# Token Fourier transform on folded halves, with v rows and gate loads placed differently, in a two-sequence encoder kernel

## The reference

```python
def fourier_mix(f):                      # f: tokens x 512 channels, 8 groups of 64
    fg = f.reshape(B, S, 8, 64)
    return jnp.fft.fftn(fg, axes=(1, 3), norm='ortho').real   # over tokens and over a group's channels

h = x @ w_in                             # f_in, q, k, v, gates
f_branch = fourier_mix(f_in) @ w_fo
a_branch = window_attention(q, k, v, sink) @ w_ao     # 8 heads, 2 kv heads, blocks of 128 tokens
merged = gates[..., :1024] * f_branch + gates[..., 1024:] * a_branch
x = layer_norm(ALPHA * x + merged @ w_out)
# peer: 128*128 = 16384 experts; 8 heads choose 16 each per token
s1, i1 = top_k(...); s2, i2 = top_k(...)              # chosen experts and softmax gates
act = gelu(x . u[eidx]); out = sum(gate * act * v[eidx])
x = layer_norm(ALPHA * x + out + ple)
```

## Time and profile before

| what | us |
|---|---|
| three runs | 3372.45, 3372.86, 3387.92 |
| median | 3372.86 |
| the profiled execution's own time | 3368.09 |
| its span, first to last instruction | 3366.2 |
| PE busy | 3206.8 (95%) |
| DVE busy | 1968.2 (58%) |
| POOL busy | 1866.5 (55%) |
| ACT busy | 1024.1 (30%) |

### The profile page before, as it was taken

How to read it: one execution, slowest core, us unless ns; L and a number is a source line. 1 busy time by engine, 2 the same in 40 slices (tenths; PEclk the granted TensorE clock), 3 DMA queues, 4 the chain that set the end, 5 groups by cost and what they waited for, 6 DMA issues and landing times.

```text
span 3366.2 us, 40493 instructions
## 1 busy us (share of the span) xinstructions
PE 3206.8 (95%) x14740; PEld 2632.9 (78%) x14740; DVE 1968.2 (58%) x3363; ACT 1024.1 (30%) x1427; POOL 1866.5 (55%) x1430
## 2 busy tenths in 40 slices
PE   7999899999999997899999999999997999999996
PEld 6677787888888886578778888888886888888885
DVE  3511315994100000854648997888885678887888
ACT  2432222333322221410102333444443223322231
POOL 3034344655544432665474332777777688888872
PEclk9999899999999999999999999999998999999998
DMA  6268678777777876598789998999999999999995
GB/s 243 91 213 274 225 243 301 242 241 240 243 238 244 252 242 226 149 347 336 257 320 350 317 326 293 371 393 394 393 394 409 353 340 340 343 354 333 346 349 180
DMA packets 322538, 988.38 MB, mean 294 GB/s; under 512 B 46896, under 2 KB 80176, under 8 KB 310960
## 3 DMA queue, kind: packets, MB, share of 16 engines
q1 hardware_dynamic: 226960, 708.80, 60.4%
q0 software_dynamic: 91264, 272.96, 22.6%
q10 hardware_dynamic: 4128, 4.19, 0.4%
HBM read 737.28 MB, written 248.51 MB: 293 GB/s over the span
## 4 chain that ended last, share of the span: by engine, by line
PE 55%; POOL 19%; issue 17%; DMA 3%; DVE 3%; another core or an unknown queue 2%; DVEq 1%; SPq 0%; ACT 0%; POOLq 0%; ACTq 0%
PE ps L1280 17%; PE ps L1282 17%; PE ps L1281 17%; POOL value L831 7%; POOL v_row L848 7%; POOL w_lo L797 4%; PE ps L1585 3%; POOL u_lo L797 1%; DMA v_row<-in_v_rows,row_i 1%; DVE acc L936 1%; DMA pair<-pair_dram 1%; DMA pair_dram<-w_lo 0%; PE ps L1503 0%; DMA u_lo<-lo_dram 0%
## 5 line engine op out<-in xcount | busy, mean ns | idle before, releaser
L1280 PE MATMUL ps<-xt_hi,w_hi 128*128 128x512 f32 (+1 forms) x2424 | 988.6, 408 | 32.0 <-issue 20.5
L848 POOL DMA_INDIRECT v_row<-in_v_rows,row_i x512 | 675.3, 1319 | 521.7 <-DVE acc L936 405.0
L1281 PE MATMUL ps<-xt_lo,w_hi 128*128 128x512 f32 (+1 forms) x2424 | 940.4, 388 | 0.0
L936 DVE SCALAR_TENSOR_TENSOR acc<-v_row,share,acc 128x1024 f32<-128x1024 f32 x512 | 658.0, 1285 | 249.7 <-DMA v_row<-in_v_rows,row_i 194.8
L1282 PE MATMUL ps<-xt_hi,u_lo 128*128 128x512 f32 x2048 | 801.4, 391 | 0.0
L831 POOL DMA_INDIRECT value<-act_dram,value_i x512 | 645.6, 1261 | 226.0 <-issue 155.7
L797 POOL TENSOR_TENSOR u_lo<-u_raw,w_hi 128x512 fp32r<-128x512 f32 x256 | 359.9, 1428 | 346.1 <-ACT w_hi L683 338.8
L1280 PEld LDWEIGHTS ps<-xt_hi,w_hi 128*128 128x128 f32 x2424 | 459.9, 190 | 110.7 <-issue 26.0
L1281 PEld LDWEIGHTS ps<-xt_lo,w_hi 128*128 128x128 f32 x2424 | 459.9, 190 | 71.2 <-issue 0.2
L1282 PEld LDWEIGHTS ps<-xt_hi,u_lo 128*128 128x128 f32 x2048 | 385.5, 188 | 82.4
L702 ACT ACTIVATE act_t<-ps 128x512 f32<-128x512 f32 x256 | 153.1, 598 | 971.9 <-PE ps L1282 888.2
(11 more groups left out here) (210 smaller groups left out, 4086.0 us busy)
## 6 DMA issues: line engine op xcount, KB each, us to landing
u_raw<-in_u_t SPq DMA_DIRECT2D x256, 512.0 KB
pair<-pair_dram SPq DMA_DIRECT2D x69, 1024.0 KB
lo_dram<-u_lo SPq DMA_DIRECT2D x128, 512.0 KB, 5.3
act_dram<-act_t SPq DMA_DIRECT2D x256, 256.0 KB
u_lo<-lo_dram SPq DMA_DIRECT2D x128, 512.0 KB
u_raw<-in_v_rows SPq DMA_DIRECT2D x128, 512.0 KB
w_raw<-in_weights SPq DMA_DIRECT2D x69, 512.0 KB, 5.2
pair_dram<-w_hi SPq DMA_DIRECT2D x69, 512.0 KB, 5.7
```

Of the source, the lines that this page charges most:

```text
L848: pool.indirect_dma_start(out=v_row[:, i % ROWS_DEEP, :], out_offset=None, in_=v_rows, in_offset=bass.IndirectOffsetOnAxis(ap=row_i[:, tt, ...
L936: dve.scalar_tensor_tensor(out=there, in0=v_row[:, i % ROWS_DEEP, :], scalar=share[:, tt, k:k + 1], in1=there, op0=ALU.mult, op1=ALU.add). ...
L1280: pe.matmul(where, lh, rh, start=first, stop=False)
L1281: pe.matmul(where, lh, rl, start=False, stop=False)
```

## The change

It has three parts.

1. **The token transform by halves.** The cosine and the sine of frequency k at token t + 256 are those at token t times (-1)^k. So for even k only the sum of the two token halves of `pq` is needed, for odd k only the difference, each over 256 tokens. After `normalise(0)` DVE now makes `pq_sum` (first half plus second half) and, after a drain, puts the difference into the second half of `pq`; both are 128x2048 operations. PE waits for these (`pq_folded`) where it waited for `pq_copied`. Each `fourier_tokens` call is four matmuls of 256 columns instead of four of 512: two of `pq_sum` with the even columns of `dft` and two of the difference with the odd ones, the columns read with a step of two. Even frequencies land in the first half of the PSUM bank and odd ones in the second; ACT (`fm`) and, for s = 0, DVE (`fm_lo`) put them in order again as they write, with a step of two on the SBUF side. `dft` is half as large and comes in two transfers of 0.5 MB.
2. **Rows.** In the sample's mix stage DVE adds 4 rows in each of units 2 to 7 where it added 3 in each of units 0 to 7; 24 both times, and no other count of rows changes.
3. **Gate groups.** ACT issues the load of `g_in` group 0 at n = 121 as before, and that of group 1 at n = 126 instead of 121.

```diff
@@ -74,7 +74,7 @@
 
 GATHERS = NT * HK
 ROWS_DEEP = 4
-START_ROWS, UNIT_ROWS = 0, 3
+UNIT_ROWS, ROWS_FROM = 4, 2
 GAP_ROWS, GAPS = 1, 10
 BATCH_ROWS, LAST_ROWS = 2, 18
 FIRST_VALUES = 18
@@ -85,7 +85,7 @@
 def rows_before(j):
 
     tiles = min(j, OUT_AT) - MERGE_AT + max(0, j - QUERY_AT)
-    return START_ROWS + UNITS * UNIT_ROWS + 2 * tiles
+    return (UNITS - ROWS_FROM) * UNIT_ROWS + 2 * tiles
 
 
 def reloaded(n):
@@ -134,7 +134,7 @@
     return ROWS_CHOICE + BATCH_ROWS * max(0, batch - 1)
 
 
-assert SEQS == 2 and FIRST_LOADS_AT + DEEP < EXPERT_TILES and EXPERT_TILES % DEEP == 0
+assert SEQS == 2 and FIRST_LOADS_AT + 5 < EXPERT_TILES and EXPERT_TILES % DEEP == 0
 
 
 def nth_norm(s, which):
@@ -208,7 +208,9 @@
         fm_lo1, o_lo1 = at("fm_lo1", 183, [P, FT, T], F32R), at("o_lo1", 98, [P, FT, T], F32R)
         fm_hi1, o_hi1 = at("fm_hi1", 167, [P, FT, T], F32R), at("o_hi1", 175, [P, FT, T], F32R)
         pq = at("pq", 114, [P, NT, 2, FOURIER])
-        dft = at("dft", 130, [P, 2, NT, T])
+
+        dft = at("dft", 130, [P, 2, NT // 2, T])
+        pq_sum = at("pq_sum", 138, [P, NT // 2, 2, FOURIER])
         m_hi, m_lo = at("m_hi", 114, [P, KD, T], F32R), at("m_lo", 130, [P, KD, T], F32R)
         gdft = at("gdft", 146, [P, 2 * P])
         fqk = at("fqk", 147, [P, 2 * FT, T])
@@ -411,7 +413,8 @@
                 sp.dma_start(gdft[:], group_dft).then_inc(mix_in, 16)
                 sp.dma_start(bias[:], attn_bias).then_inc(mix_in, 16)
                 load_layer(s, 8, MERGE_AT)
-                sp.dma_start(dft[:], token_dft.rearrange("c (t p) n -> p c t n", p=P)).then_inc(dft_in, 16)
+                for c in range(2):
+                    sp.dma_start(dft[:, c], token_dft[c, 0:T // 2].rearrange("(t p) n -> p t n", p=P)).then_inc(dft_in, 16)
                 load_ln(3 if s else 1)
                 load_layer(s, MERGE_AT, MERGE_AT + 6)
                 if s:
@@ -615,7 +618,8 @@
                     if u % 2:
                         c = u // 2
                         act.wait_ge(fm_ps, FT * s + c + 1)
-                        act.activation((fm1 if s else fm_hi0)[:, c, :], ps[:, 7, :], ACT.Copy).then_inc(fm_copied, 1)
+                        act.activation((fm1 if s else fm_hi0)[:, c, :].rearrange("p (k b) -> p b k", b=2),
+                                       ps[:, 7, :].rearrange("p (b k) -> p b k", b=2), ACT.Copy).then_inc(fm_copied, 1)
                     outputs(u)
 
                 if s:
@@ -750,11 +754,11 @@
                     if n == EXPERT_TILES - 1:
                         split_v(0)
                     gelu(n)
-                    if n == FIRST_LOADS_AT:
+                    if n in (FIRST_LOADS_AT, FIRST_LOADS_AT + 5):
                         act.wait_ge(g_stored, 16 * PIECES)
-                        for group in range(2):
-                            rows = slice(group * G_GROUP, (group + 1) * G_GROUP)
-                            act.dma_start(g_in[group][:], g_dram[:, :, rows, :].rearrange("c j i t -> j c i t")).then_inc(g_back[group], 16)
+                        group = (n - FIRST_LOADS_AT) // 5
+                        rows = slice(group * G_GROUP, (group + 1) * G_GROUP)
+                        act.dma_start(g_in[group][:], g_dram[:, :, rows, :].rearrange("c j i t -> j c i t")).then_inc(g_back[group], 16)
                     if n == NORM_PROMPT_AT:
                         deviation(4, prompt_norms)
                         prompt_norms += 1
@@ -1099,8 +1103,6 @@
                                           ps[rows, 3, :].rearrange("p (a b q) -> p a b q", a=2, b=2)[:, :, half, :],
                                           o_hi0[rows, 2 * g:2 * g + 2, cols_of(blk)].bitcast(F32), ALU.subtract).then_inc(o_lo_made, 1)
 
-                if s:
-                    add_rows(START_ROWS)
                 dve.wait_ge(mix_in, 32 * (s + 1))
                 scores(0)
                 dve.wait_ge(v_ps, s + 1)
@@ -1108,16 +1110,24 @@
                     dve.tensor_copy(v_dup[:, :, :, dup, :], ps[:, 3, :].rearrange("p (t g d) -> p t g d", t=NT, g=KV_HEADS)).then_inc(v_copied, 1)
                 for u in range(UNITS):
                     normalise(u)
+                    if u == 0:
+
+                        dve.wait_ge(pq_copied, 2 * NT * (s + 1))
+                        dve.tensor_tensor(pq_sum[:], pq[:, 0:NT // 2], pq[:, NT // 2:NT], ALU.add)
+                        dve.drain()
+                        dve.tensor_tensor(pq[:, NT // 2:NT], pq[:, 0:NT // 2], pq[:, NT // 2:NT], ALU.subtract).then_inc(pq_folded, 1)
                     if u and s == 0:
                         outputs_lo(u - 1)
                     if u + 1 < UNITS:
                         scores(u + 1)
-                    if s:
+                    if s and u >= ROWS_FROM:
                         add_rows(UNIT_ROWS)
                     if u % 2 and s == 0:
                         c = u // 2
                         dve.wait_ge(fm_copied, c + 1)
-                        dve.tensor_tensor(fm_lo0[:, c, :], ps[:, 7, :], fm_hi0[:, c, :].bitcast(F32), ALU.subtract).then_inc(fm_lo_made, 1)
+                        there = [fm[:, c, :].rearrange("p (k b) -> p b k", b=2) for fm in (fm_lo0, fm_hi0)]
+                        dve.tensor_tensor(there[0], ps[:, 7, :].rearrange("p (b k) -> p b k", b=2), there[1].bitcast(F32),
+                                          ALU.subtract).then_inc(fm_lo_made, 1)
                 if s == 0:
                     outputs_lo(UNITS - 1)
                 else:
@@ -1405,15 +1415,17 @@
                 def fourier_tokens(c, part):
 
                     if c == 0 and part == 0:
-                        pe.wait_ge(dft_in, 16 * (s + 1))
+                        pe.wait_ge(dft_in, 32 * (s + 1))
                     if c and part == 0:
                         if s:
                             pe.wait_ge(fm_copied, FT + c)
                         else:
                             pe.wait_ge(fm_lo_made, c)
-                    for tt in range(NT):
-                        mm = pe.matmul(ps[:, 7, :], pq[:, tt, part, cols_of(c)], dft[:, part, tt, :],
-                                       start=(part == 0 and tt == 0), stop=(part == 1 and tt == NT - 1))
+                    for odd, folded in enumerate((pq_sum[:], pq[:, NT // 2:NT])):
+                        for t in range(NT // 2):
+                            mm = pe.matmul(ps[:, 7, odd * T // 2:(odd + 1) * T // 2], folded[:, t, part, cols_of(c)],
+                                           dft[:, part, t, :].rearrange("p (k b) -> p b k", b=2)[:, odd, :],
+                                           start=(part == 0 and odd == 0 and t == 0), stop=(part == 1 and odd == 1 and t == NT // 2 - 1))
                     if part:
                         mm.then_inc(fm_ps, 1)
 
@@ -1436,7 +1448,7 @@
                     if u + 1 < UNITS:
                         scores(u + 1)
                     if u == 0:
-                        pe.wait_ge(pq_copied, 2 * NT * (s + 1))
+                        pe.wait_ge(pq_folded, s + 1)
                         pe.wait_ge(v_copied, 2 * (s + 1))
                     g, seen = u % 2, key_tiles(u // 2)
                     pe.wait_ge(probs_made, UNITS * s + u + 1)
```

More of the change, by code:

```diff
@@ L284, in encoder @@
         v_t_copied, v_ps = sem("v_t_copied"), sem("v_ps")
-        dft_in = sem("dft_in")
+        dft_in, pq_folded = sem("dft_in"), sem("pq_folded")
         v_copied = sem("v_copied")
```

## The result

The changed kernel takes 3402.59 us, median of ten runs (3391.56 to 3410.58); the kernel before, in ten runs beside it, 3380.85 (3368.69 to 3396.76). The ratio is 1.0057, 95% interval 1.0039 to 1.0075: slower by 13 to 25 us. I therefore compare stages, and look for what repeats in several traces.

A forecast was written before the change was run, and what follows sets the result against it. PE, busy 95% of the span, idles in mix stages behind a DVE and ACT chain and at the up tiles' end behind ACT's blocking issues. +2 + 6.3 - 11 = -2.7 from 3372.9: 3370 us, range 3352 to 3381.

The forecast's parts named there:

- The prompt's folds: Prompt mix stage: two DVE folds move PE's transposes 4.5 us later; merge +2 us, between -0.4 and +3.
- its tail: Prompt, after the last transposes: the halved transform saves 1.66 us up to the merge.
- Folds and rows, sample: Sample mix stage: folds +0.9 us at scores(3), five longer row batches +6.6 less 0.45; merge +6.3 (4.8 to 7.5).
- Three rows take 4.04 us ... They lie on DVE's path: Sample mix stage: rows cost DVE 1.33 us each; one more in each of five batches, +6.6 us.
- The 20.03 us themselves stay: nothing of the change is ahead of them: Start of the sample's mix stage: PE's 20.03 us wait for DVE's first probabilities stays unchanged.
- The gate groups: End of up tiles: ACT's block goes, down tile 0 starts 11 us sooner (6 to 18), DMA limiting the gain.
- what they carried by 2631 and need not have: End of up tiles: 4.2 MB of DMA traffic not needed by then, worth 10.7 us at 392 GB/s.
- B: End of up tiles: DMA doesn't bind, full gain of 20 to 23 us, 3357 to 3361; chance 0.22.
- C: End of up tiles: ACT's second issue blocks again at n = 126, gain 0 to 3 us, 3378 to 3380; chance 0.13.
- E: Mix stages: step-of-two access costs extra in `fm` copies and `dft` reads, some +6 us, 3377; chance 0.08.
- D: Prompt units: idle gaps bring PE's clock low, 1.5 us in each of 14 units, +20, 3390; chance 0.05.
- 16 x 1.66 us of work less: Mix stages: halved transform cuts PE's work by 26.6 us, of which only 3.4 to 5 us are seen.

The follow-up runs named there:

- part 1: Kernel before with only the folds and halved transform; three rows in each of eight units, both gate groups at n = 121: 3375.14 us, ratio 1.0013.
- parts 1 and 2: Changed kernel with both gate groups back at n = 121, folds, halved transform and four rows kept: 3390.04 us, ratio 1.0050.
- POOL's run broken up: Changed kernel with 30 first values spread three to an input tile, rows 9 to 20 without a value beside them: 3368.71 us, ratio 0.9963.
- without folds: Kernel before with the halved transform reading pq's halves unfolded, three rows per unit, both gate groups at n = 121: 3368.76 us, ratio 0.9979.
- part 3 alone: Kernel before with only the second gate group's load moved to n = 126: 3366.90 us, ratio 0.9987.
- the one with more values: Kernel before with two values instead of one gathered beside each of the mix stage's 24 rows: 3423.44 us, ratio 1.0118.
- that with 12 values: Kernel before with 12 instead of 18 values gathered ahead of the first row: 3515.98 us, ratio 1.0387.

## Why the prediction was wrong

It forecast -2.7 us and no measurable change (3352 to 3381), with 0.04 for slower; measured were +22 by the medians, +13 to +25 by the ratio.

**The prompt's folds: right in DVE's part, its tail too cheap.** By line and form the changed kernel's trace has (ns min/median/max)

```profile
L1116 DVE TENSOR_TENSOR pq_sum<-pq x2: 2284/2284/2284, 107.1 to 1361.8; 128x2048 f32<-128x2048 f32 x2
...
L1426 PE MATMUL ps<-dft,pq_sum x64: 385/388/635, 113.5 to 1451.0; 128*128 128x256 f32 x64
...
L621 ACT ACTIVATE fm_hi<-ps x4: 597/608/629, 128.4 to 182.4; 128x512 fp32r<-128x512 f32 x4
```

and the second fold takes 2.29 us. With them the transposes are 4.2 us later, for 4.5. Scores to scores stayed at 9.8 us, and a call of the transform takes 1.8 us. The merge is 3.3 us later in the trace (2.9 in those of part 1 and of parts 1 and 2), just outside the range of -0.4 to +3: the last transform, which was to save 1.66 us, ran at the low clock, its four records at 178.78 in 1.89 us where those at 1370.03 took 1.09.

**Folds and rows, sample: the step that failed.** It was the sentence that counts the rows by DVE alone: "Three rows take 4.04 us ... They lie on DVE's path". I gave the sample's merge +6.3, of which 4.4 lie ahead of its first transposes and 1.9 behind them. The sum was right for DVE: with POOL's run broken up, start to merge is +1.9. What I left out is POOL. Four rows are 8 issues of some 1.25 us or more, 10 to 11 us in a unit of 10 to 11.6, so POOL's pauses vanish, and PE's increments come late. That costs 6 to 8 us more from unit 6 on (+7.5 and +9.5 where +1.9 was summed), shown by taking the run away and by making it longer. The sum has no term for POOL at all. The sentence "The 20.03 us themselves stay: nothing of the change is ahead of them" held in the traces of the parts (19.4 us without folds, 23.2 and 23.3 with them, 4.4 more being summed for the folds). It did not in the changed kernel's: 28.90 us, 4.5 more than folds explain, with `v_ps` 3.2 us behind the end of POOL's run where it came 1.2 us ahead of it before. The trace without folds has the same lateness, `v_ps` 3.3 us behind and 24.5 us of idle time, so these 4.5 us come and go from one trace to another and not with the folds. I had not asked what the 20 us were; they were the same mechanism, in plain view before, with its price on it.

**The gate groups: mechanism right, size off.** The issues take 0.4 us each; the idle time moved to tiles 125 to 127 and to down tile 0, as forecast, with DMA behind it; only it was the load of `g_in`, and not of `act_in`, that came last. Forecast were -11 at down tile 0. Counted from the lag that each trace had in its up tiles 16 to 112, by ACT's activations (+0.8 us for part 3, +44.8 for the changed kernel), part 3 alone had -6.0 there and -2.2 at PE's last matmul, the changed kernel -7.7 and -4.2. The median of part 3 is -4.4 (-9 to 0). The term was missing its second half: "what they carried by 2631 and need not have" is carried later, and the down stage had no room for it. Its DMA share of 96% was in the trace before.

**The rivals.** B is refuted by the 8 us before down tile 0, C by the 0.37 us issue. E: the `fm` copy takes 608 ns against 572, and a matmul record with its step of two 388, what a plain one of 256 columns takes (379), so steps of two cost next to nothing. By the Trainium skill, "Advanced Engine Details and Errata", section SBUF Cachelines, two hits in a line run at full speed, and the two rows agree but for 36 and 9 ns. D, the clock, has a part, though not in each unit as it was thought: low time in the trace is 161 us against 126, partly in stretches behind the new waits, and PE is busy in 71 us of it against 50. At half the clock this is some 11 us of PE's time, as an estimate. It is a part of why PE's busy time fell by 8 us only (3206.8 to 3198.5), where 16 x 1.66 us of work less were summed.

**What stays open.** PE in the changed kernel's trace lags that of before by 3.3 us at the prompt's merge, 8.6 at the prompt's last up tile, 17.3 at the sample's first transposes, 26.8 at its merge, 44.8 in its up tiles (by ACT's activations), 37.1 at down tile 0 and 40.6 at the end. POOL's issues account for some 12 of the 40 us: 4.5 ahead of the sample's first transposes and 7.6 up to its merge. Two other steps are not accounted for. In five traces with folds the prompt's last up tile is 4.8 to 8.6 us later than before, in eleven without them -1.4 to +6.2; the mix stage explains 3 to 5, the rest I could not place. From the sample's merge to its first up tiles the changed kernel takes 16 us more, the one with more values 24, that with 12 values 30, the others -8 to +9, with no rule by kind of kernel. In the changed kernel about 9 of the 16 are idle time of PE and 7 are PE busy for longer at a lower granted clock (0.95 against 0.97). Over all traces POOL's runs there have up to 84 issues. The kernel before has runs of 22 and 24 issues in these tiles too, from 1489 to 1562, and no idle time of 1 us in them. Why a run does harm in one execution or stage and not in another isn't settled; the mix stage, where each unit goes through three engines and back, is where a run of 16 or more inside it did so every time. Which part of the chip holds PE's increments back can't be read from these traces either.

## What to carry to other kernels

An engine that only issues can hold others back: before adding issues to one, measure the longest stretch without a pause, and look at what others wait for inside it. A wait whose releaser the profile doesn't name, on engines whose producer has finished, is worth an experiment that lengthens and shortens what runs beside it; here that gave 23 us that no part of the change had been after. And when DMA engines are full from a place to the end, count a removed byte, not a removed wait.

## What the runs showed of the hardware

While POOL issues indirect DMAs 0.30 us apart, PE's semaphore increments arrive late: in the changed kernel 7 to 10 us in a run of 16 issues, at the start of the mix stage up to 23 us in a run of 28 (`v_t`'s transposes ended at 1335.9, `v_ps` was raised at 1359.08) and 34 us in one of 44. They come one by one there, 4 to 7 us apart in the run of 28 and up to 11 in that of 44. At 3.6 us into the changed kernel's run of 16 an increment still came at once. A run of 12 issues (17 us) did nothing measurable in the traces of three rows. ACT's and DVE's increments were not seen to lag. The Trainium skill, "SBUF — State Buffer", section SBUF: two separate sides, tells of DVE holding up the DMAs that POOL issues; what these runs show goes the other way, and touches PE.
